# Layer norms by token halves in a five-layer transformer kernel

## The chip, the cores and the metric

The kernel runs on one core of one Trainium2 chip. The metric is the device time of one execution in microseconds (us), and the time given is the median of several executions.

TensorE (PE in the rows, its weight loads PEld) multiplies matrices, VectorE (DVE), ScalarE (ACT) and GpSimd (POOL) work on tiles, and SyncE (SP) issues transfers. Each works through its own list of instructions in order and waits at semaphores for the others.

## The reference

A first transformer block is followed by four more, all in float32 on 512 tokens of width 1024. What matters here is the frame of the four later layers:

```python
for i in range(4):
    h = x * (1 + scale[0]) + shift[0]
    y = mixer_i(h)                    # mLSTM, windowed attention, HGRN2, differential attention
    x = layer_norm(ALPHA * x + (1 + gate[0]) * y, ln_g[i, 0], ln_b[i, 0])
    h = x * (1 + scale[1]) + shift[1]
    y = (silu(h @ w_gate) * (h @ w_up)) @ w_down
    x = layer_norm(ALPHA * x + (1 + gate[1]) * y, ln_g[i, 1], ln_b[i, 1])

def layer_norm(x, g, b, eps=1e-5):    # over the 1024 channels of each token
    mu = x.mean(-1); var = square(x - mu).mean(-1)
    return (x - mu) * rsqrt(var + eps) * g + b
```

So there are eight layer norms: one after each output projection (the last step of `mixer_i`), one after each down projection. Each token is normed by itself, and each needs all 1024 channels of that token.

## The kernel before

**Layout.** Everything is kept transposed: 128 partitions hold channels, the free axis holds the 512 tokens. `x` has eight chunks `x[:, c, :]` of 128 channels (DT = 8). A result tile `m` of a projection is 128 output channels by 512 tokens in one of eight PSUM banks; tiles go round banks 0 to 3, and a tile may start when the one four before it has been evicted (`lin_free`).

**Products.** For float32 accuracy each operand is split in a high part of 32-bit matmul type and the rest. A chunk of a tile is three products, high by high, high by low, low by high (lines 756 to 758 in `slot_products`). A tile of the output projection has 8 chunks, so 24 products; one of the down projection has 22 chunks, so 66.

**Weights.** They come in slots of 8 chunks (512 KB): a DMA fills `raw`, ScalarE copies it to `w_hi` (L1440, `split`), GpSimd subtracts to get `w_lo` (L623, `low`). Each of the three has a ring of 4 slots (RING), and ScalarE may write a slot again when TensorE has used it (`slot_used`). An output or input tile has 1 slot, a down tile 3. ScalarE's list is written so that it splits 4 slots ahead (LEAD) of the tile in hand.

**Residual.** In `add_gated` VectorE adds each finished tile to `x` (L2062) and to a running sum over channels (L2066). ScalarE squares `x` (L1513), VectorE adds the squares (L2079), so that after the last tile little is left: add tile 7, square it, add the square.

**Layer norm.** `layer_norm` on TensorE sums over the partitions with a matrix of ones, one column per 128 tokens (L897, 8 float32 products, two records each). VectorE and ScalarE make mean, variance, root and inverse (L1988 to L1996, L1517), TensorE spreads the inverse and the mean times it over the partitions (L917, 8 products), VectorE multiplies (L1979) and subtracts (L1983) for each chunk of `x`. In between TensorE runs idle products (L903), which compute nothing. For each chunk ScalarE then writes `h_hi` (L1524) and `h_tmp` (L1526), and GpSimd `h_lo` (L661):

```python
act.wait_ge(sm.ln_y, (n["ln"] - 1) * DT + c + 1)
fn(h_hi[:, c, :], x[:, c, :], ACT.Identity, bias=..., scale=...).then_inc(sm.part_hi, 1)
fn(h_tmp[:, c, :], x[:, c, :], ACT.Identity, bias=..., scale=...).then_inc(sm.h_ready, 1)
```

**Early tiles.** The next projection does not wait for all of `h`. `early_tiles` runs the first three tiles (EARLY) together, chunk by chunk: six products with `h_hi[c]` (L854, L855), then three with `h_lo[c]` (L859). After its 16 writes ScalarE scales the residual in eight operations (L1530, `x_scaled`). Only behind these stand the next split of a slot (the one for tile 4) and, after an output projection, the table load and the first SiLU of the feed-forward part (L1800, in `ffn`). Tile 3 needs one slot more than the three early ones, and it is split right after the root.

The last norm of the program has no projection behind it: ScalarE writes `x` (L1537, `normed_output`), and each chunk is stored by a DMA of 256 KB.

**Third attention.** In the fourth layer `diff_attention` puts its scores in banks 1, 2 and 3 in turn, and the norm after it takes its sums in bank 0 (`NORM_SUMS[3]`).

Of the kernel before, what the change touches and what calls it, by code (L numbers as in the profile page):

```python
# [8 lines left out]
F32 = mybir.dt.float32  # L9
# [7 lines left out]
P = 128  # L17
S = 512
# [75 lines left out]
NORM_SUMS = {"first": 7, 0: 2, 3: 0}  # L94
# [69 lines left out]
PARTS_SPLIT = 3 * DT + FT  # L164

# [16 lines left out]
def lin_total(parts):  # L182

    return sum(len(IN_PROJ[p][0]) + len(IN_PROJ[p][1]) + 2 * DT + 2 * FT for p in parts)
# [34 lines left out]
def program(nc, xT, wstream, ada, cond, cols, kept, bigc, layerc, pos, yT, parts):  # L219
    slots_total = stream_length(parts)  # L220
    ctx = ExitStack()
    with ctx:
# [117 lines left out]
        def col(name, j=0, n=1):  # L340
# [37 lines left out]
                 "ln_var_done", "ln_root", "ln_inv", "ln_spread", "ln_times", "ln_y", "ln_x",  # L378
# [139 lines left out]
        LN_ORDER = [4, 0, 1, 2, 3, 5, 6, 7]  # L518
# [17 lines left out]
        def _(sp):  # L536
# [75 lines left out]
            for c in range(DT):  # L612
                if parts[-1] != "first":
                    sp.wait_ge(sm.ln_x, c + 1)
                sp.dma_start(yT[:, c, :], x[:, c, :]).then_inc(sm.stored, 16)
            sp.wait_ge(sm.stored, 16 * DT)
# [3 lines left out]
        def _(pool):  # L620
# [33 lines left out]
            def input_low(tile, scaled, chunks=range(DT)):  # L654

                for c in chunks:
                    n.add(part=1, h=1 if scaled else 0)
                    if scaled:
# [3 lines left out]
                                            ALU.subtract).then_inc(sm.part_lo, 1)  # L662

# [34 lines left out]
            for at, part in enumerate(parts):  # L698
# [6 lines left out]
                else:  # L705
# [10 lines left out]
                    else:  # L716
                        low_to(first_slot + LEAD)
                        input_low(lambda c: h_tmp[:, c, :], True)
# [19 lines left out]
                low_to(first_slot + inputs + DT + LEAD)  # L738
                input_low(lambda c: h_tmp[:, c, :], True)
# [6 lines left out]
        def _(pe):  # L746
# [124 lines left out]
            def residual_tiles(done, hi, lo, chunks, sums, parts_from=None):  # L871
# [3 lines left out]
                summed = 0  # L875
                for q in range(done, DT + 1):
# [7 lines left out]
                n.add(slot=(DT - done) * per, mt=DT - done)  # L884
# [9 lines left out]
            def token_sums(out, src):  # L894

                for t in range(TT):
                    op = mm(out[:, t:t + 1], src[:, t * P:(t + 1) * P], ones[:, 0:1], start=True, stop=True)  # L897
                return op
# [6 lines left out]
            def layer_norm(total, squares):  # L905

                pe.wait_ge(sm.lin_free, n["mt"] - 1)
                idle_products((n["mt"] - 2) % 4, 2)
                pe.wait_ge(sm.lin_free, n["mt"])
                token_sums(bank[6], total).then_inc(sm.ln_sum, 1)  # L910
                pe.wait_ge(sm.ln_moment, n["ln"])
                token_sums(bank[5], squares).then_inc(sm.ln_sum, 1)
                idle_products((n["mt"] - 1) % 4, 1)
                for at, src in enumerate((ln_rstd, ln_drop)):
                    pe.wait_ge(sm.ln_inv, 2 * n["ln"] - 1 + at)
                    for t in range(TT):
                        op = turn(bank[4 + 3 * at][:, t * P:(t + 1) * P], src[:, t:t + 1].to_broadcast([P, P]), ident)  # L917
                    op.then_inc(sm.ln_spread, 1)
                idle_products((n["mt"] - 1) % 4, 3)
# [142 lines left out]
            def diff_attention():  # L1062
                a, g, items = n["att"], n["att_g"], out_norms(3)
                for step in range(len(DF_UNITS) + 3):
                    if step < len(DF_UNITS):
                        hd, i = DF_UNITS[step]
                        w = (i + 1) * P
                        for c in range(2):
# [3 lines left out]
                            mm(bank[1 + (2 * step + c) % 3][:, 0:w], proj[:, hd, i * P:(i + 1) * P],  # L1072
# [297 lines left out]
            def ffn(sums):  # L1370
                early_tiles()
                linear(2 * FT - EARLY, h_hi, h_lo, [8])
                residual_tiles(0, hid_hi, hid_lo, [8, 8, 6], sums, parts_from=n["part"])
                n.add(part=FT)

            pe.wait_ge(sm.const_loaded, 48)
            for at, part in enumerate(parts):
# [8 lines left out]
                else:  # L1386
                    early_tiles()
                    if part == 0:
                        mlstm_gates()
                    linear(len(tiles) - EARLY, h_hi, h_lo, [8])  # L1390
# [24 lines left out]
                residual_tiles(EARLY, h_hi, h_lo, [8], sum_squares if part == "first" else pivot(sums_out[0]))  # L1415
                if part != "first":
# [1408 lines left out]
```

## Time and profile before

| | us |
|---|---|
| median of 3 runs | 3290.86 |
| lowest, highest | 3290.30, 3292.92 |
| profiled execution, its span | 3288.7 |
| TensorE busy in it | 3220.8 |
| VectorE, ScalarE, GpSimd busy | 1549.8, 1202.1, 1480.9 |

For the profiled execution the profile gives the span of the instructions, 3288.7 us, and no time of its own beside it. The span is 2.1 us under the median of the runs; what lies around the instructions is taken to be that.

Times in the rows below are microseconds from the start of the span, unless "mean ns" is said. In a timeline the first number is the start, the second the time from there to the end of the last instruction that the row joins (xN). A matmul's stated length is longer than its distance to the next, because matmuls overlap; the distance between starts is what it costs in a stream.

### The profile page before, as it was taken

Reading aid. Unit: us, or ns where it says so; the run is one execution under the profiler, and the core shown is the slowest. Engines: PE = TensorE matmul, PEld = TensorE weight load, DVE = VectorE, ACT = ScalarE, POOL = GpSimd, SP = SyncE. Lnnn points to the kernel's source line nnn. Section 1 sums busy time; section 2 is a strip of 40 time slices with the busy share of each in tenths; the row PEclk is TensorE's granted clock in tenths of the full one; section 3 lists DMA queues with packets and bytes.
Section 4 is the critical chain, followed back from the end, with each engine's and each line's share of the span. In section 5 each row is a group of like instructions: output and inputs, shape, how many; then the busy total and the mean of one; then the engine's idle time right before and its main releaser. Section 6 shows DMA issues by size and latency. Waiting matters only on the chain.

```text
span 3288.7 us, 42736 instructions
## 1 busy us (share of the span) xinstructions
PE 3220.8 (98%) x15181; PEld 2619.6 (80%) x15181; DVE 1549.8 (47%) x2615; ACT 1202.1 (37%) x1875; POOL 1480.9 (45%) x724
## 2 busy tenths in 40 slices
PE   8999999999999999999999999999999999999998
PEld 6876788888778888887888878877888877788886
DVE  2453355501145555467555224656556354752223
ACT  3455333222335332455432243125332243553322
POOL 3540554454235445524544454446444453154442
PEclk9999999999999999999999999999999999999999
DMA  4400155532224554211556333113555322032331
GB/s 161 122 26 1 65 204 191 202 106 93 68 65 160 193 202 145 84 59 63 180 191 208 105 96 96 39 33 103 204 191 188 103 90 77 5 99 96 96 103 64
DMA packets 103107, 376.12 MB, mean 114 GB/s; under 512 B 11456, under 2 KB 11584, under 8 KB 102848
## 3 DMA queue, kind: packets, MB, share of 16 engines
q1 hardware_dynamic: 102816, 373.86, 34.1%
q8 instruction: 81, 1.33, 0.2%
q0 software_dynamic: 160, 0.52, 0.1%
q14 instruction: 50, 0.41, 0.0%
HBM read 372.24 MB, written 2.10 MB: 114 GB/s over the span
## 4 chain that ended last, share of the span: by engine, by line
PE 52%; DVE 2%; ACT 1%; issue 1%; POOL 0%; DVEq 0%; ACTq 0%
PE bank L758 13%; PE bank L757 13%; PE bank L756 13%; PE bank L1362 2%; PE bank L859 1%; PE bank L854 1%; PE bank L855 1%; PE bank L808 1%; PE bank L809 1%; PE bank L810 1%; PE bank L1072 1%; PE bank L1328 1%; PE bank L1089 0%; PE bank L974 0%; PE bank L1258 0%
## 5 line engine op out<-in xcount | busy, mean ns | idle before, releaser
L623 POOL TENSOR_TENSOR w_lo<-raw,w_hi 128x1024 fp32r<-128x1024 f32 x501 | 1227.3, 2455 | 1368.2 <-ACT w_hi L1440 1368.0
L1440 ACT ACTIVATE w_hi<-raw 128x1024 fp32r<-128x1024 f32 x501 | 526.8, 1057 | 1183.2 <-PE bank L758 1022.4
L756 PE MATMUL bank<-h_hi,w_hi 128*128 128x512 f32 x2280 | 889.3, 390 | 0.0
L758 PE MATMUL bank<-h_hi,w_lo 128*128 128x512 f32 x2280 | 887.1, 389 | 0.0
L757 PE MATMUL bank<-h_lo,w_hi 128*128 128x512 f32 x2280 | 887.0, 389 | 0.0
L756 PEld LDWEIGHTS bank<-h_hi,w_hi 128*128 128x128 f32 x2280 | 427.9, 188 | 90.6 <-issue 2.0
L757 PEld LDWEIGHTS bank<-h_lo,w_hi 128*128 128x128 f32 x2280 | 427.9, 188 | 89.7 <-issue 1.0
L758 PEld LDWEIGHTS bank<-h_hi,w_lo 128*128 128x128 f32 x2280 | 427.9, 188 | 89.2
L2608 DVE CUSTOM_DVE_ANT_0 ada_raw<-ada_raw,cond_row 128x1024 f32<-128x1024 f32 x192 | 304.2, 1587 | 280.5 <-DMA ada_raw<-ada 270.6
L756 PE MATMUL bank<-hid_hi,w_hi 128*128 128x512 f32 x880 | 344.0, 391 | 0.0
L758 PE MATMUL bank<-hid_hi,w_lo 128*128 128x512 f32 x880 | 342.4, 389 | 0.0
L757 PE MATMUL bank<-hid_lo,w_hi 128*128 128x512 f32 x880 | 342.4, 389 | 0.0
L2624 DVE TENSOR_TENSOR hid_lo<-layer_const,hid_hi 128x512 f32 (+1 forms) x110 | 228.0, 2073 | 108.5 <-ACT hid_hi L1805 108.5
L661 POOL TENSOR_TENSOR h_lo<-proj,h_hi 128x512 fp32r<-128x512 f32 x40 | 55.7, 1407 | 308.5 <-ACT h_hi L1472 308.5
L757 PEld LDWEIGHTS bank<-hid_lo,w_hi 128*128 128x128 f32 x880 | 165.2, 188 | 35.3 <-issue 1.0
L756 PEld LDWEIGHTS bank<-hid_hi,w_hi 128*128 128x128 f32 x880 | 165.2, 188 | 35.1 <-issue 1.0
L758 PEld LDWEIGHTS bank<-hid_hi,w_lo 128*128 128x128 f32 x880 | 165.2, 188 | 34.3
L1800 ACT ACTIVATE layer_const<-bank 128x512 f32<-128x512 f32 x110 | 65.7, 597 | 321.1 <-PE bank L758 317.0
L2062 DVE SCALAR_TENSOR_TENSOR x<-bank,mod,x 128x512 f32<-128x512 f32 x64 | 48.0, 750 | 264.4 <-PE bank L758 255.7
L2621 DVE TENSOR_TENSOR layer_const<-bank,layer_const 128x512 f32<-128x512 f32 x110 | 75.9, 690 | 201.0 <-PE bank L758 163.4
L854 PE MATMUL bank<-h_hi,w_hi 128*128 128x512 f32 x336 | 135.5, 403 | 1.3 <-ACT h_hi L1472 1.0
L855 PE MATMUL bank<-h_hi,w_lo 128*128 128x512 f32 x336 | 131.9, 393 | 0.0
(411 smaller groups left out, 4016.5 us busy)
## 6 DMA issues: line engine op xcount, KB each, us to landing
raw<-weights SPq DMA_DIRECT2D x501, 512.0 KB, 3.5
ada_raw<-ada SPq DMA_DIRECT2D x192, 512.0 KB, 4.3
layer_const<-layer_const SPq DMA_DIRECT2D x5, 512.0 KB, 3.6
x<-x_t SPq DMA_DIRECT2D x1, 2048.0 KB, 7.5
cond_row<-cond SPq DMA_DIRECT2D x4, 512.0 KB, 4.2
y_t<-x SPq DMA_DIRECT2D x8, 256.0 KB, 2.0
tables<-big_const SPq DMA_DIRECT2D x1, 768.0 KB, 5.9
cols<-columns SPq DMA_DIRECT2D x1, 569.5 KB, 8.4
```

The source lines that it names most:

```text
L623: nc.gpsimd.tensor_tensor(w_lo[k % RING][:, :, :], raw[k % RING][:, :, :], w_hi[k % RING][:, :, :].bitcast(F32), ALU.subtract).then_inc(sm ...
L756: mm(out, w_hi[r][:, at, :], hi, start=first and at == 0, stop=False)
L757: mm(out, w_hi[r][:, at, :], lo, start=False, stop=False)
L758: op = mm(out, w_lo[r][:, at, :], hi, start=False, stop=last and at == len(pairs) - 1)
L854: mm(out, w_hi[r][:, c, :], h_hi[:, c, :], start=c == 0, stop=False)
L855: mm(out, w_lo[r][:, c, :], h_hi[:, c, :], start=False, stop=False)
L1362: op = mm(bank[3 + m % 3][:, j * P:(j + 1) * P], kk[:, j * P:(j + 1) * P], qq[:, j * P:(j + 1) * P], start=True, stop=True)
L1440: fn(w_hi[t % RING][:, :, :], raw[t % RING][:, :, :], ACT.Copy).then_inc(sm.hi_done, 1)
L1800: fn(sil[q % 2], bank[(mt + 2 * q) % 4][:, :], ACT.Silu).then_inc(sm.sil_done, 1)
L2608: v.tensor_tensor_reduce(w, w, cond_row[:, :], 1.0, 0.0, ALU.mult, ALU.add, ada_part[:, kc:kc + 1]).then_inc(sm.ada_used, 1)
L2621: v.tensor_tensor(sil[q % 2], bank[(mt + 2 * q + 1) % 4][:, :], sil[q % 2], ALU.mult).then_inc(sm.lin_free, 2)
L2624: v.tensor_tensor(hid_lo[:, q + 4 * i, :], sil[q % 2], hid_hi[:, q + 4 * i, :].bitcast(F32), ALU.subtract).then_inc(sm.part_lo, 1)
```

## The change

1. Tokens are cut into two halves of 256. The last tile (7) of an output or down projection is computed as two half tiles, first all chunks for tokens 0 to 255, then all chunks for tokens 256 to 511 (`half_tile`), in two banks.
2. The norm of half 0 stands inside the second half tile on TensorE: after chunk 3, 7 and 8 (output) or 6, 12 and 13 (down) come the sums and the two spreads. The idle products go, but for the last norm of the program.
3. The three early tiles are run by halves (`early_halves`): eight chunks for half 0, then eight for half 1. For chunks 0 to 2 of half 0 only two tiles are run, the third tile catches up after chunk 2. After chunk 3 of half 0 TensorE makes the sums of half 1, after chunk 5 its spreads.
4. ScalarE, VectorE and GpSimd do the norm by halves: 32 writes of `h` with 256 columns in place of 16 with 512, 32 of VectorE's operations in place of 16, 16 of GpSimd's in place of 8. Each has a fixed order in which both halves' steps, and the splits of slots, are mixed.
5. The residual is scaled as before, 8 times 512 columns, after all 32 writes.
6. The output is stored in 16 DMAs of 128 KB in place of 8 of 256 KB.
7. Since each norm's last tile now takes two banks, the count of tiles shifts; in the fourth layer the scores go to banks 0, 1 and 3 and the sums to bank 2.

The core of the diff (waits and signals of other functions left out):

```diff
-NORM_SUMS = {"first": 7, 0: 2, 3: 0}
+NORM_SUMS = {"first": 7, 0: 2, 3: 2}
+TAIL = {"out": (7,), "down": (7,)}
...
+            def half_tile(k, mt, hi, lo, chunks, half, after=lambda: None):
+                cols = half_cols(half)
+                out = bank[mt % 4][:, cols]
...
+                    for at in range(m):
+                        mm(out, w_hi[r][:, at, :], hi[:, c, cols], start=c == 0, stop=False)
+                        mm(out, w_hi[r][:, at, :], lo[:, c, cols], start=False, stop=False)
+                        op = mm(out, w_lo[r][:, at, :], hi[:, c, cols], start=False, stop=c == last)
+                        if half == 1 and at == m - 1:
+                            op.then_inc(sm.slot_used, 1)
...
+                        at = (6, 12, 13) if per > 1 else (3, 7, 8)
+                        if passed == at[0]:
+                            half_sums(0, tail, *norm)
+                        elif passed in at[1:]:
+                            half_spread(0, at.index(passed) - 1)
...
+            def early_halves(tail, total, squares):
...
+                        if half == 0 and c == LN_CHUNK - 1:
+                            for before in range(LN_CHUNK):
+                                high(0, before, EARLY - 1)
+                                low(0, before, EARLY - 1)
+                        if half == 0 and c == 3:
+                            half_sums(1, tail, total, squares)
+                        if half == 0 and c == 5:
+                            for at in range(2):
+                                half_spread(1, at)
...
+            def normed_low(first):                      # GpSimd
+                low_to(first + 2)
+                half_low(0)
+                low_to(first + 3)
+                for c in range(1, DT):
+                    half_low(c)
+                low_to(first + LEAD)
+                for c in range(DT):
+                    later_low(c)
...
+                for _ in tail:                          # ScalarE, end of layer_norm
+                    square()
+                root(0)
+                split_ahead(1)
+                apply(0, 0)
+                if slots > 1:
+                    split_ahead(1)
+                apply(0, 1)
+                square()
+                for c in (2, 3):
+                    apply(0, c)
+                root(1)
+                for c in range(4, DT):
+                    apply(0, c)
+                if slots > 1:
+                    split_ahead(1)
+                for c in range(DT):
+                    apply(1, c)
...
+                second_half(7)                          # VectorE, end of add_gated
+                for c in (3, 4):
+                    apply(0, c)
+                moments(1)
+                apply(0, 5)
+                inverses(1)
+                apply(0, 6)
+                apply(0, 7)
+                for c in range(DT):
+                    apply(1, c)
...
-                            mm(bank[1 + (2 * step + c) % 3][:, 0:w], proj[:, hd, i * P:(i + 1) * P],
+                            mm(bank[(0, 1, 3)[(2 * step + c) % 3]][:, 0:w], proj[:, hd, i * P:(i + 1) * P],
```

**ScalarE at the first output projection's norm.** Before: `bank<-x` are the squares, `ln_small` the root, `w_hi` a split, `h_hi` and `h_tmp` the writes of `h`, in brackets the semaphores waited for.

```order
L1440 ACTIVATE w_hi_59<-raw_55 128x1024 [waits slot_used,raw_loaded1]
L1513 ACTIVATE bank<-x 128x512 [waits ln_added,ln_residual] x2
L1517 ACTIVATE ln_small<-ln_small,kept 128x4 [waits ln_var_done]
L1440 ACTIVATE w_hi_60<-raw_56 128x1024 [waits slot_used,raw_loaded2]
L1524 ACTIVATE h_hi<-x,ln_cols 128x512 [waits ln_y]
```

The same place after the change, from the root of half 0 to that of half 1 (`sq_88` is the square of the last tile's second half):

```order
L1695 ACTIVATE ln_small<-ln_small,kept 128x2 [waits ln_var_done]
L1613 ACTIVATE w_hi_60<-raw_56 128x1024 [waits slot_used,raw_loaded2]
L1731 ACTIVATE h_hi<-x,ln_cols 128x256 [waits ln_y]
L1733 ACTIVATE h_tmp<-x,ln_cols 128x256
L1731 ACTIVATE h_hi<-x,ln_cols 128x256 [waits ln_y]
L1733 ACTIVATE h_tmp<-x,ln_cols 128x256
L1688 ACTIVATE sq_88<-x 128x256 [waits ln_residual]
L1731 ACTIVATE h_hi<-x,ln_cols 128x256 [waits ln_y]
L1733 ACTIVATE h_tmp<-x,ln_cols 128x256
L1731 ACTIVATE h_hi<-x,ln_cols 128x256 [waits ln_y]
L1733 ACTIVATE h_tmp<-x,ln_cols 128x256
L1695 ACTIVATE ln_small<-ln_small,kept 128x2 [waits ln_var_done]
```

A second root now stands between the fourth and the fifth pair of writes, and the 24 other writes stand behind it.

**GpSimd at the same norm.** Before, the slots 0, 1 and 2 of the early tiles and slot 3 are all made low before the first `h_lo`:

```order
L623 TENSOR_TENSOR w_lo_62<-raw_54,w_hi_58 128x1024 [waits hi_done]
L622 REGISTER_ALU
L623 TENSOR_TENSOR w_lo_63<-raw_55,w_hi_59 128x1024 [waits hi_done]
L622 REGISTER_ALU
L623 TENSOR_TENSOR w_lo_64<-raw_56,w_hi_60 128x1024 [waits hi_done]
L199 REGISTER_ALU
L199 COMPARE_AND_BRANCH
L661 TENSOR_TENSOR h_lo<-h_tmp,h_hi 128x512 [waits part_hi,h_ready] x8
```

After (here `w_lo_65` and `w_lo_62` are the slots of the first two early tiles, `w_lo_63` that of the third, `w_lo_64` that of tile 3):

```order
L654 TENSOR_TENSOR w_lo_65<-raw_57,w_hi_61 128x1024 [waits hi_done]
L654 TENSOR_TENSOR w_lo_62<-raw_54,w_hi_58 128x1024 [waits hi_done]
L701 TENSOR_TENSOR h_lo<-h_tmp,h_hi 128x256 [waits half_hi,half_tmp]
L654 TENSOR_TENSOR w_lo_63<-raw_55,w_hi_59 128x1024 [waits hi_done]
L701 TENSOR_TENSOR h_lo<-h_tmp,h_hi 128x256 [waits half_hi,half_tmp] x7
L654 TENSOR_TENSOR w_lo_64<-raw_56,w_hi_60 128x1024 [waits hi_done]
L710 TENSOR_TENSOR h_lo<-h_tmp,h_hi 128x256 [waits part_hi,h_ready] x8
```

The low part of the third early tile's slot has moved behind the first half chunk, that of tile 3's slot behind the eighth.

## Rows read from the trace of the kernel before

**Rows 1.** The page: engines over the whole span; shares of the chain.

```profile
PE 3220.8 (98%) x15181; PEld 2619.6 (80%) x15181; DVE 1549.8 (47%) x2615; ACT 1202.1 (37%) x1875; POOL 1480.9 (45%) x724
PE 52%; DVE 2%; ACT 1%; issue 1%; POOL 0%; DVEq 0%; ACTq 0%
```

**Rows 2.** Windows, the seven norms with a projection behind: length, then engines, clock.

```profile
995.02:1003.66 8.64, 8.31 (x37) 5.81 (x36) 5.73 (x13) 3.28 (x6) 2.36 (x1) 0.80 0.39 137
...
1550.47:1558.03 7.56, 7.18 (x38) 4.54 (x36) 5.17 (x12) 2.71 (x5) 2.32 (x1) 1.00 0.40 156
...
sum 55.84, PE 53.59 PEld 35.32 DVE 37.57 ACT 20.39 POOL 16.34; mean PE 7.66 PEld 5.05 DVE 5.37 ACT 2.91 POOL 2.33
```

**Rows 3.** Timeline of TensorE, second layer's output norm.

```profile
1550.24 0.39 PE L758 MATMUL bank<-h_hi,w_lo 128*128 128x512 f32 x1
...
1552.14 1.95 PE L897 MATMUL bank<-kept,sums_out 128*128 128x1 f32 x16 [0.21 <-DVE sums_out L2066]
...
1558.03 0.50 PE L854 MATMUL bank<-h_hi,w_hi 128*128 128x512 f32 x1
```

**Rows 4.** Timeline of VectorE, same norm: a square added, a subtraction.

```profile
1548.74 0.69 DVE L2079 TENSOR_TENSOR sums_out<-sums_out,bank 128x512 f32<-128x512 f32 x1
...
1550.67 0.75 DVE L2062 SCALAR_TENSOR_TENSOR x<-bank,mod,x 128x512 f32<-128x512 f32 x1 [1.24 <-PE bank L758]
```

**Rows 5.** Timeline of ScalarE, same norm, from the first write of h.

```profile
1557.16 0.81 ACT L1524 ACTIVATE h_hi<-x,ln_cols 128x512 fp32r<-128x512 f32 x1 [1.52 <-DVE x L1983]
...
1568.48 5.75 ACT L1530 ACTIVATE x<-x,ln_cols 128x512 f32<-128x512 f32 x8
1574.24 1.28 ACT L1800 ACT_TABLE_LOAD   x1
1575.54 0.60 ACT L1800 ACTIVATE layer_const<-bank 128x512 f32<-128x512 f32 x1
1576.03 2.00 ACT L1440 ACTIVATE w_hi<-raw 128x1024 fp32r<-128x1024 f32 x2
```

**Rows 6.** Timeline of GpSimd, same norm.

```profile
1558.76 12.83 POOL L661 TENSOR_TENSOR h_lo<-h_tmp,h_hi 128x512 fp32r<-128x512 f32 x8 [0.68 <-ACT h_tmp L1526]
1577.16 7.58 POOL L623 TENSOR_TENSOR w_lo<-raw,w_hi 128x1024 fp32r<-128x1024 f32 x3 [5.57 <-ACT w_hi L1440]
```

**Rows 7.** Window of the same norm's three early tiles.

```profile
1558.03:1575.20 17.17, 16.75 (x73) 13.54 (x73) 12.20 (x17) 17.15 (x24) 12.20 (x9) 1.00 0.18 62
```

**Rows 8.** Groups by form over the span: busy, mean ns of one | idle before.

```profile
L1615 ACT ACTIVATE df_p<-df_p,small 128x512 f32<-128x512 f32 x16 | 11.3, 711 | 0.0
L1615 ACT ACTIVATE df_p<-df_p,small 128x256 f32<-128x256 f32 x16 | 7.9, 496 | 0.0
L2342 DVE TENSOR_TENSOR st_e<-st_z,bank 128x256 f32<-128x256 f32 x4 | 1.7, 414 | 0.0
L649 POOL TENSOR_TENSOR hg_k<-hg_k,hg_pow 128x128 f32<-128x128 f32 x8 | 3.4, 427 | 3.0 <-PE bank L1356 3.0
```

**Rows 9.** TensorE: products of 256 columns, of 128 columns, and the page's weight load.

```profile
131.20 0.28 PE L1153 MATMUL bank<-w_hi,blk_parts 128*64 128x256 f32 x1
131.32 0.28 PE L1153 MATMUL bank<-w_lo,blk_parts 128*64 128x256 f32 x1
...
1432.27 0.27 PE L826 MATMUL bank<-w_lo,h_hi 128*128 128x128 f32 x1
1432.38 0.28 PE L827 MATMUL bank<-w_hi,h_lo 128*128 128x128 f32 x1
...
L756 PEld LDWEIGHTS bank<-h_hi,w_hi 128*128 128x128 f32 x2280 | 427.9, 188 | 90.6 <-issue 2.0
```

**Rows 10.** Timeline of ScalarE, second layer's down norm, after its writes.

```profile
1936.83 5.74 ACT L1530 ACTIVATE x<-x,ln_cols 128x512 f32<-128x512 f32 x8
1943.31 2.96 ACT L1440 ACTIVATE w_hi<-raw 128x1024 fp32r<-128x1024 f32 x3 [0.74 <-PE bank L859]
```

**Rows 11.** Timeline of ScalarE, last norm: the last write before its store.

```profile
3285.48 0.81 ACT L1537 ACTIVATE x<-x,cols 128x512 f32<-128x512 f32 x1 [0.51 <-DVE x L1983]
```

More of the change, by code:

```diff
@@ L182, in lin_total @@
 def lin_total(parts):
-    return sum(len(IN_PROJ[p][0]) + len(IN_PROJ[p][1]) + 2 * DT + 2 * FT for p in parts)
+    return sum(len(IN_PROJ[p][0]) + len(IN_PROJ[p][1]) + 2 * DT + 2 * FT +
+               (0 if p == "first" else len(TAIL["out"]) + len(TAIL["down"])) for p in parts)
 class Counts(dict):
@@ L869, in early_tiles, with residual_tiles @@
                 early_done()
-            def residual_tiles(done, hi, lo, chunks, sums, parts_from=None):
+            def half_tile(k, mt, hi, lo, chunks, half, after=lambda: None):
+                cols = half_cols(half)
+                out = bank[mt % 4][:, cols]
+                pe.wait_ge(sm.lin_free, mt - 3)
+                c, last = 0, sum(chunks) - 1
+                for s, m in enumerate(chunks):
+                    if half == 0:
+                        pe.wait_ge(sm.lo_done, k + s + 1)
+                    r = (k + s) % RING
+                    for at in range(m):
[4 more added lines that the diff above has]
+                            op.then_inc(sm.slot_used, 1)
+                        if half == 0 and c == last:
+                            op.then_inc(sm.half_tile, 1)
+                        c += 1
+                        after()
+            def residual_tiles(done, hi, lo, chunks, sums, parts_from=None, tail=(), norm=None):
                 k, mt, per = n["slot"], n["mt"], len(chunks)
-                summed = 0
-                for q in range(done, DT + 1):
+                summed, whole = 0, DT - len(tail)
+                for q in range(done, whole if tail else DT + 1):
                     if q < DT:
@@ L892, in pivot, with token_sums @@
                 return add
-            def token_sums(out, src):
-                for t in range(TT):
-                    op = mm(out[:, t:t + 1], src[:, t * P:(t + 1) * P], ones[:, 0:1], start=True, stop=True)
+            def token_sums(out, sources, half):
+                for t in range(2):
+                    for at, src in enumerate(sources):
+                        op = mm(out[:, 2 * half + t:2 * half + t + 1], src[:, t * P:(t + 1) * P], ones[:, 0:1],
+                                start=at == 0, stop=at == len(sources) - 1)
                 return op
```

372 lines of the change are left out of this document (250 added, 122 removed).

## The prediction

> **What bounds the kernel now.** I read the page first. TensorE is busy for 98% of the span and the chain that ended last is mostly its own [rows 1], so the end moves only where TensorE computes nothing of use, or gets to compute less. Idle products count as busy, so that share hides the norms. The windows between the last product of a last tile and the first early product show them: seven, 55.84 us together, 7.56 each with the clock granted in full and about 8.6 in the three in which 0.80 was granted [rows 2]. The early tiles behind a norm take 17.17 us [rows 7], where 72 products at a distance of 0.227 (24 of them fill the 5.46 us of a tile) make 16.4. An eighth norm ends the program. So some 60 us are there to be had. What could take their place is read from ScalarE: in the early tiles it was busy for 17.15 of 17.17 us [rows 7]. It has no room there, and what it does next, scaling the residual, ends with the table load at the very moment when it is wanted [rows 5].
>
> **Prices.** A norm is followed in us from Ta, the start of the last tile: 1545.01 in the second layer's output projection, which is the last product's start plus 0.23 less 5.46 [rows 3]. Half products: the trace has 256 columns at a distance of 0.12 and, with weights of 128 columns, 128 columns at 0.11 [rows 9]; I take 0.114, so that two halves cost no more than a whole. ScalarE: the eight operations of 5.75 us start 0.707 apart and last 0.80 [rows 5]; its form of 256 columns is 0.215 shorter than that of 512 [rows 8], so a half write is 0.59 long and 0.49 apart. That puts 32 of them at 15.8 us, against 16 × 0.707 = 11.3. Bounds: 0.35 if all of the cost went with the columns, 0.55 if a third of the saving were missing; I take 0.49, since the measured pair of forms has just this step. VectorE: 256 columns 0.41 [rows 8], a pair of multiply and subtract about 0.79; 16 pairs 12.6 us, in the shadow of ScalarE. GpSimd: 128 columns 0.43 [rows 8], 512 unhindered 1.30 (8 of them span 12.83 us, ScalarE's pace in between [rows 6]), so 0.74 for 256; bounds 0.65, half of 1.30, and 0.90. A slot's low part 2.4 (three in 7.58 us [rows 6]). Float32 sums: 16 records in 1.95 us [rows 3], 0.112 each; a half's 6 products have 12, so 1.3 us, and both spreads of a half 0.44. TensorE thus does 2 × (1.3 + 0.44) = 3.5 us of norm work that it cannot overlap with products; this takes the place of the idle ones and of waiting.
>
> ScalarE's price is also one that the Trainium skill states: "ScalarE: Activation LUTs", section What ACT_TABLE_LOAD costs, has an operation with pointers for bias and scale at 372 ns plus 0.833 ns a column, less 93 ns when back to back. By it a half write is 0.585 long and 0.492 apart; the trace has 0.80 for 512 columns, where the rule gives 0.799. It speaks against halving: each cut in two buys 0.28 us of fixed cost again.
>
> **An output norm.** 2.74: half tile 0 is done. VectorE is not there yet: it adds tile 6's square until 1549.43, or 4.4 [rows 4]. Two half additions (0.48 long, 0.40 apart) end at 5.2; TensorE, which stands before the sums with three chunks of half 1 made, has waited 1.5 for them. Sums to 6.6, 15 products and the spreads to 8.8. ScalarE's next split waits for the tile's slot, free only at the end of half 1: 8.7 to 9.7. Then it starts to write `h`: 9.7 against 12.15 before [rows 5]. That is all that is won, 2.4 us.
> ScalarE reaches the second root at 13.9 (four pairs, one square). That root waits for the sums of half 1, which TensorE makes behind chunk 3. Chunk 1 needs its `h_lo`, and on GpSimd the third early tile's slot stands ahead of it: chunk 0's `h_lo` ends at 11.6, the slot at 14.0, chunk 1 at 14.7. TensorE has waited 2.5. Then chunks 1 to 3 and the third tile's nine products run to 17.9, the sums to 19.2, the variance to 19.5: ScalarE has stood for 5.6. TensorE waits 1.25 until chunk 4 comes, 0.6 for its `h_lo`, and again 1.6 at the start of half 1, where GpSimd has tile 3's slot (24.6 to 27.0) ahead of the `h_lo`. The early tiles end at 35.5, against 30.2 before.
> ScalarE, in order: 9.7 + 15.8 of writes + 0.5 square and root + 5.6 + 0.7 (its wait for the spreads) = 32.3. Then eight residuals 5.66, to 38.0; the table load 1.28, to 39.3, no longer hidden; SiLU 0.49; the split for tile 4, 1.05, to 40.8; its low part 2.4, to 43.3. TensorE ended tile 3 at 35.5 + 5.46 = 41.0 and waits 2.3. Before, tile 4 began at 1580.64, or 35.6. So 7.7 us slower; in the two output norms with the clock at 0.80, where it began about 0.6 later, 7.1. Behind it nothing gives it back: the feed-forward part is TensorE's at 5.46 a tile. Four such norms: 2 × 7.7 + 2 × 7.1 = 29.6.
>
> **A down norm.** Its tile has 66 products, 15.0 us, and VectorE is free. Half 0 ends at 7.5; its sums, wanted 2.05 later, are ready for, and its norm hides behind half 1, which ends at 16.8 with 1.8 of sums and spreads in it. ScalarE writes the first half chunk at 14.4, before the tile is done. Three splits now lie between its steps, each behind a slot that half 1 has to free. GpSimd's low part of the third slot (16.5 to 18.9) again holds up chunk 1, by 1.75, ScalarE stands for 4.6 at the second root, and TensorE waits 1.25 for chunk 4, 0.6, and 1.8 at half 1's first `h_lo`. The early tiles end at 40.6 (39.7 before). ScalarE: 14.4 + 15.8 + 0.5 + two splits 1.9 + 4.6 + 0.2 = 37.5; residuals to 43.2, split to 44.2, low part to 46.7. Before, ScalarE's residuals were over 0.74 us ahead of need [rows 10], and tile 4 began at 45.2. So 1.5 slower, 1.0 in the norm with the lower clock: 2 × 1.5 + 1.0 = 4.0.
>
> **The last norm.** Before, the last write starts 16.6 us after the last tile's last product and 3.3 before the end [rows 11]. Now half 1 ends 1.8 later, VectorE does two left pairs (1.6), moments and three pairs more before half 1's eight (6.3); the last write ends at Ta + 29.7, in place of Ta + 32.4. The stores are half as large but twice as many; the last alone counts, and I price it as before (bounds: 1 us less, half the transfer; 1 us more, queued behind others). So 2.7 gained.
>
> **Banks of the third attention**, the shifted tile banks, the waits added before the residuals (on ScalarE's own signals): nothing, since the same number of banks turn in the same order. If a bank were shared with a running tile, one eviction, 0.7 us, would come in.
>
> Sum: 29.6 + 4.0 − 2.7 = 30.9 us on the span of 3288.7; with the 2.1 us between span and median, 3290.9 + 31 = 3322 us.
>
> **Rivals.**
> A, faster. The waits of ScalarE at the second root do not come, because the sums of half 1 are there when it is. Then the output norm's tile 4 begins at 43.3 − 6.3 = 37.0, 1.4 slower or 0.8; a down norm is bound by TensorE, 16.8 + 16.4 + 1.8 + 5.46 = 40.5, rounded up by one wait of 0.5 to 41.0, so 4.2 faster; with the last norm 4.4 − 13.1 − 2.7, or about −11: 3280. For it: VectorE and ScalarE do start earlier. Against it: the order on GpSimd, written into its list.
> B, slower by less. The early tiles end late as worked out, but residuals, SiLU and the split find room: only 2 × 5.3 + 2 × 4.7 + 2.2 (down) − 2.7 = 19.5 remain: 3310. Against it stands that ScalarE was without slack before.
> C, slower by more. The clock falls to 1.2 GHz in these scattered waits, as in the three norms at 0.80, or VectorE's work slows GpSimd's half chunks to 0.90. A stretch at 0.80 was 1.0 us longer [rows 2]; twice in seven norms 14: 3336.
> D. A weight load is not hidden behind a half product. Then half products pass 0.188 apart [rows 9] in place of 0.114: 192 of them in an output norm, 14 us, 276 in a down norm, 20, and 132 at the end, 10; together 126, of which some 20 fill waits. That gives 3322 + 105 = 3427. This is what the Trainium skill would have, "TensorE: Matmul & The Clock Gate", section The mechanism: loads overlap running products only when they are in other row groups. The trace speaks against it: full loads with 128 columns pass 0.11 apart.
>
> **How the numbers follow.** Forecast 0.56, with its own range 3312 to 3332: the bounds of a half write move an output norm by −2 and +1 and a down norm by −2 and +1.5, those of GpSimd by up to 1. A 0.12, B 0.14, C 0.16, D 0.02. The range that should hold the time 8 times in 10 reaches over most of B and C: 3302 to 3341. What this kernel's measurement can tell from no change is about 0.2%, or 6.6 us: faster by more, 0.10 (most of A); within it, 0.05 (A's rest and a bit of B); slower, 0.85.
>
> **What would show it.** ScalarE's half writes about 0.49 apart; its second root behind 4 to 6 us of idle; GpSimd's low part of the third slot between the first and the second half chunk, and TensorE idle for 2 us before the second `h_lo`; residual operations that end after the early tiles; a wait of TensorE for `w_lo` before tile 4 in each feed-forward part. I am wrong if tile 4 starts within 1 us of the end of tile 3, or if the early tiles behind an output norm end less than 31 us after Ta.

## The result, and the profile after

The changed kernel takes 3351.7 us (median of 4 runs, 3347.9 to 3353.1), the kernel before 3290.6 in the same session: a ratio of 1.0186, 95% interval 1.0171 to 1.0200, +61 us. I had forecast 3322, +31, with a range up to 3341. The sign and the place were right, the size was half.

The page of the profiled execution (span 3346.1), the lines that answer to [rows 1]:

```profile
PE 3234.1 (97%) x16021; PEld 2677.5 (80%) x16021; DVE 1563.5 (47%) x2791; ACT 1241.9 (37%) x2011; POOL 1487.1 (44%) x780
...
PE 48%; DVE 3%; ACT 2%; issue 2%; POOL 1%; DVEq 0%; POOLq 0%; ACTq 0%
```

TensorE is busy for 13 us more and the span is 57 us longer; so it waits, and part of its work is slower. The next windows go from Ta, the start of the last tile, to the start of tile 4. Columns: length, busy time of PE, PEld, DVE, ACT, POOL, granted clock, DMA share, GB/s; `...` stands where rows are left out. First the second layer's output norm and down norm, the sum of all seven, then a stretch inside the output norm.

```profile
1558.76:1606.64 47.88, 39.11 (x249) 36.36 (x247) 24.22 (x59) 31.88 (x56) 22.65 (x21) 0.85 0.16 56
1931.38:1979.91 48.53, 44.58 (x334) 42.57 (x332) 20.74 (x55) 31.15 (x53) 23.65 (x22) 0.96 0.18 55
...
sum 336.73, PE 288.50 PEld 270.98 DVE 163.47 ACT 221.03 POOL 160.19; mean PE 41.21 PEld 38.71 DVE 23.35 ACT 31.58 POOL 22.88
...
1565.52:1582.00 16.48, 12.47 (x68) 11.64 (x68) 6.02 (x19) 5.91 (x13) 5.12 (x5) 0.70 0.19 65
```

Before, this output norm took 35.6 and the down norm 45.2. The stretch at 0.70 is new: in the kernel before the clock was granted in full there [rows 2, 7].

TensorE in that output norm (last half product before the sums, the sums, half 1 behind them, the first early product, its waits for chunk 1's `h_lo` and for chunk 4, then the end of tile 3 and tile 4):

```profile
1562.60 0.28 PE L946 MATMUL bank<-h_hi,w_lo 128*128 128x256 f32 x1
1564.01 0.83 PE L998 MATMUL bank<-kept,sums_out 128*128 128x1 f32 x6 [1.14 <-DVE sums_out L2279]
...
1565.88 0.41 PE L945 MATMUL bank<-h_lo,w_hi 128*128 128x256 f32 x1
1566.09 0.41 PE L946 MATMUL bank<-h_hi,w_lo 128*128 128x256 f32 x1
...
1570.86 0.38 PE L1046 MATMUL bank<-h_hi,w_hi 128*128 128x256 f32 x1 [1.48 <-ACT h_hi L1731]
...
1575.18 0.80 PE L1051 MATMUL bank<-h_lo,w_hi 128*128 128x256 f32 x2 [1.37 <-POOL h_lo L701]
...
1582.55 0.58 PE L1046 MATMUL bank<-h_hi,w_hi 128*128 128x256 f32 x1 [1.15 <-ACT h_hi L1731]
...
1603.66 0.39 PE L820 MATMUL bank<-h_hi,w_lo 128*128 128x512 f32 x1
1606.64 0.79 PE L818 MATMUL bank<-h_hi,w_hi 128*128 128x512 f32 x1 [2.59 <-POOL w_lo L654]
1607.23 0.63 PE L819 MATMUL bank<-h_lo,w_hi 128*128 128x512 f32 x1
```

Up to 1562.60 half products pass 0.12 apart. Then TensorE stands for 1.14, makes sums of one column, and the next half products pass 0.21 apart (1565.88 to 1566.09): that is the level of 1.2 GHz. The same happens behind the 2.59 us before tile 4, whose first products are 0.4 to 0.6 apart instead of 0.227.

ScalarE, from the first write of `h`; the row at 1587.60 is the first write of half 1, the last row is the second root of the second layer's down norm:

```profile
1570.22 0.59 ACT L1731 ACTIVATE h_hi<-x,ln_cols 128x256 fp32r<-128x256 f32 x1
1570.71 0.59 ACT L1733 ACTIVATE h_tmp<-x,ln_cols 128x256 f32<-128x256 f32 x1
...
1581.71 0.30 ACT L1695 ACTIVATE ln_small<-ln_small,kept 128x2 f32<-128x2 f32 x1 [7.13 <-DVE ln_small L2207]
...
1587.60 0.60 ACT L1731 ACTIVATE h_hi<-x,ln_cols 128x256 fp32r<-128x256 f32 x1 [1.64 <-DVE x L2197]
...
1595.54 5.76 ACT L1741 ACTIVATE x<-x,ln_cols 128x512 f32<-128x512 f32 x8
1601.32 1.28 ACT L2011 ACT_TABLE_LOAD   x1
1602.61 0.60 ACT L2011 ACTIVATE layer_const<-bank 128x512 f32<-128x512 f32 x1
1603.11 2.00 ACT L1613 ACTIVATE w_hi<-raw 128x1024 fp32r<-128x1024 f32 x2
...
1956.58 0.30 ACT L1695 ACTIVATE ln_small<-ln_small,kept 128x2 f32<-128x2 f32 x1 [4.50 <-DVE ln_small L2207]
```

This is the chain of the forecast: half writes 0.59 long and 0.49 apart, a root that waits, residuals behind the writes, then table load, SiLU and the split for tile 4, none of them hidden any longer [rows 5].

GpSimd in the output norm: chunk 0's low part, the slot's, chunks 1 to 3; and the last three of half 1.

```profile
1571.38 0.73 POOL L701 TENSOR_TENSOR h_lo<-h_tmp,h_hi 128x256 fp32r<-128x256 f32 x1 [9.74 <-ACT h_tmp L1733]
1572.07 2.38 POOL L654 TENSOR_TENSOR w_lo<-raw,w_hi 128x1024 fp32r<-128x1024 f32 x1
1574.40 2.10 POOL L701 TENSOR_TENSOR h_lo<-h_tmp,h_hi 128x256 fp32r<-128x256 f32 x3
...
1593.73 3.79 POOL L710 TENSOR_TENSOR h_lo<-h_tmp,h_hi 128x256 fp32r<-128x256 f32 x3 [0.26 <-ACT h_tmp L1733]
```

The last write of the program, against [rows 11], 2.7 us before the end of the span and 29.85 after its Ta of 3313.53:

```profile
3343.38 0.60 ACT L1748 ACTIVATE x<-x,cols 128x256 f32<-128x256 f32 x1 [0.19 <-DVE x L2197]
```

**Where the 57.4 us between the two spans lie.** From Ta to tile 4: output norms +10.2, +12.2, +12.7, +12.2, together 47.3; down norms +2.9 to +3.5, together 9.8. The feed-forward parts behind tile 4 took 324.7 to 324.9 us instead of 323.2: 6.5, the slow first products of tile 4. Last norm −2.2. All other stretches −4.0: −2.7 before the first of these norms, +1.8 and −3.3 in the attention and HGRN2 layers, where single stretches at the lower clock come and go from one execution to the next. The fourth layer's stage with the swapped banks took 233.4 against 233.2.

### The profile page after: what moved, and what is told of

Same layout as the page of the kernel before. It is cut to its first block, busy times and chain, and to the rows that moved or that the text cites. A ratio compares the mean times of both kernels' runs of the same rounds, so it can differ in the third digit from the quotient of the medians.

```text
span 3346.1 us, 44788 instructions
## 1 busy us (share of the span) xinstructions
PE 3234.1 (97%) x16021; PEld 2677.5 (80%) x16021; DVE 1563.5 (47%) x2791; ACT 1241.9 (37%) x2011; POOL 1487.1 (44%) x780
## 4 chain that ended last, share of the span: by engine, by line
PE 48%; DVE 3%; ACT 2%; issue 2%; POOL 1%; DVEq 0%; POOLq 0%; ACTq 0%
PE bank L818 11%; PE bank L820 11%; PE bank L819 11%; PE bank L1524 2%; PE bank L870 1%; PE bank L872 1%; PE bank L1234 1%; PE bank L871 1%; ACT h_hi L1731 1%; ACT h_tmp L1733 1%; PE bank L944 1%; PE bank L946 1%; PE bank L945 1%; PE bank L921 1%; PE bank L916 1%
## 5 line engine op out<-in xcount | busy, mean ns | idle before, releaser
L818 PE MATMUL bank<-h_hi,w_hi 128*128 128x512 f32 x2248 | 880.6, 392 | 15.1 <-POOL w_lo L654 15.1
L820 PE MATMUL bank<-h_hi,w_lo 128*128 128x512 f32 x2248 | 876.6, 390 | 0.0
L818 PE MATMUL bank<-hid_hi,w_hi 128*128 128x512 f32 x792 | 309.7, 391 | 0.0
L820 PE MATMUL bank<-hid_hi,w_lo 128*128 128x512 f32 x792 | 308.2, 389 | 0.0
L819 PE MATMUL bank<-hid_lo,w_hi 128*128 128x512 f32 x792 | 308.2, 389 | 0.0
L819 PEld LDWEIGHTS bank<-hid_lo,w_hi 128*128 128x128 f32 x792 | 148.7, 188 | 31.9 <-issue 1.0
L820 PEld LDWEIGHTS bank<-hid_hi,w_lo 128*128 128x128 f32 x792 | 148.6, 188 | 30.9
L2276 DVE SCALAR_TENSOR_TENSOR x<-bank,mod,x 128x512 f32<-128x512 f32 (+1 forms) x72 | 49.7, 690 | 235.0 <-PE bank L820 199.1
L1046 PE MATMUL bank<-h_hi,w_hi 128*128 128x256 f32 x336 | 97.9, 313 | 13.6 <-ACT h_hi L1731 13.6
L2016 ACT ACTIVATE hid_hi<-layer_const 128x512 f32 (+1 forms) x110 | 68.3, 621 | 94.9 <-DVE layer_const L2869 94.9
```

Of the source, the lines that this page charges most:

```text
L818: mm(out, w_hi[r][:, at, :], hi, start=first and at == 0, stop=False)
L819: mm(out, w_hi[r][:, at, :], lo, start=False, stop=False)
L820: op = mm(out, w_lo[r][:, at, :], hi, start=False, stop=last and at == len(pairs) - 1)
L1046: mm(out, w_hi[r][:, c, :], h_hi[:, c, cols], start=c == 0, stop=False)
L2016: fn(hid_hi[:, q + 4 * i, :], sil[q % 2], ACT.Copy).then_inc(sm.part_hi, 1)
```

## The experiments

Twelve kernels, each timed beside the kernel before. Differences to the changed kernel are taken across sessions; the median of the kernel before was 3289.8 to 3290.6 in all of them. The columns out and down are the time from Ta to tile 4 in the second layer's output and down norm. The edits are shown abridged.

| kernel | out | down | median, us | ratio to before (95%) |
|---|---|---|---|---|
| before | 35.6 | 45.2 | 3290 | |
| changed | 47.9 | 48.5 | 3351.7 | 1.0186 (1.0171 to 1.0200) |
| idle | 59.5 | 54.8 | 3412.5 | 1.0377 (1.0362 to 1.0391) |
| resid | 45.4 | 47.2 | 3328.5 | 1.0115 (1.0100 to 1.0131) |
| root | 45.8 | 44.5 | 3327.2 | 1.0116 (1.0101 to 1.0132) |
| all3 | 58.2 | 54.7 | 3404.9 | 1.0350 (1.0335 to 1.0364) |
| fill | 43.8 | 47.9 | 3326.5 | 1.0113 (1.0097 to 1.0128) |
| rr | 43.2 | 45.1 | 3316.0 | 1.0086 (1.0072 to 1.0099) |
| rrgf | 38.8 | 44.2 | 3295.4 | 1.0014 (1.0005 to 1.0023) |
| noidle | 36.9 | 47.7 | 3300.4 | 1.0033 (1.0021 to 1.0046) |
| down0 | 36.4 | 48.2 | 3298.0 | 1.0025 (1.0016 to 1.0035) |
| down1 | 35.9 | 44.2 | 3287.4 | 0.9990 (0.9981 to 0.9999) |
| pool | 47.5 | 52.2 | 3358.3 | 1.0210 (1.0197 to 1.0224) |
| all4 | 38.0 | 44.4 | 3293.7 | 1.0012 (1.0003 to 1.0021) |

My theory after the result: the chain was as forecast, and what I had not priced is the clock, which the removed idle products had kept. The rivals: the halves cost more everywhere, or one of the waits in the chain is much worse than worked out.

**idle.**

```diff
+    idle_products(bank that is free, FILL[...])   # 384 columns, ahead of five waits of a norm
```

> The changed kernel with idle products (384 columns, nothing computed) in the waits that its trace shows: in an output norm 6 before the sums of half 0, 8 before the first early product, 7 before chunk 1's low part, 6 before chunk 4, 14 before tile 4; in a down norm 7, 6 and 7 at the last three. Theory 1, the fallen clock costs the part I had not priced: granted clock stays at 1.00 in the output norms, ScalarE's wait at the second root falls from 7.1 to about 4, half products pass 0.12 apart everywhere, tile 4 starts 3.4 earlier and itself runs 1.7 faster: about 3330. Rival, the half products and waits at ScalarE's pace lower the clock whatever stands between them, or the pace of ScalarE alone counts: 3346 to 3355.

Measured 3412.5, 61 us slower. I had mis-sized the filler. The window of the second output norm:

```profile
1578.22:1637.68 59.46, 59.06 (x332) 46.54 (x330) 25.92 (x60) 33.09 (x57) 29.09 (x23) 1.00 0.22 75
```

The clock is 1.00 as expected, but TensorE is busy for all 59 us: each product stands as two records 0.32 apart, 0.645 us, and 41 of them are 26 us in place of the five waits' 7.7 us in this norm (1.14, 1.48, 1.37, 1.15 and 2.59). So the clock can be held; of the time this kernel says nothing. The same holds for all3.

**resid.**

```diff
 with up to q = 3 of the first round of SiLUs unrolled:
     up(q, 0)
+    scaled_residual((2 * q, 2 * q + 1))
 next layer: for c in range(DT):
     split_ahead(1)
+    scaled_residual((c,))
```

> The changed kernel with the eight scalings of the residual spread behind the next splits, two by two behind SiLUs in the feed-forward part, one behind each split of the next layer's input projection, so that SiLU and split for tile 4 follow the last half write directly. Theory 1: the wait before tile 4 (2.6 in an output norm, 3.4 in the last, 1.3 in a down norm) goes, and with it the dip of the clock at its end (1.7 in an output norm): 3351.7 - 10.4 - 3.9 - 6.8, about 3331. Rival, the split waits for the slot that the early tiles free, and its low part behind it is late all the same: over 3345.

Measured 3328.5, −23. TensorE at the start of tile 4 (1602.16) no longer waits:

```profile
1601.93 0.39 PE L820 MATMUL bank<-h_hi,w_lo 128*128 128x512 f32 x1
1602.16 0.41 PE L818 MATMUL bank<-h_hi,w_hi 128*128 128x512 f32 x1
```

So the wait before tile 4 is ScalarE's residual standing ahead of the split, as predicted. In the traces tile 4 comes 8.5 us earlier over the four output norms and 4.4 over the three down norms, and itself takes 5.5 instead of 7.0 behind an output norm. The clock in the output norms stayed low (0.85 in three, 0.78 in the fourth), so apart from tile 4's own 1.5 us this gain is the chain's, not the clock's.

**root.**

```diff
-    if half == 0 and c == 3:     # sums of half 1
+    if half == 0 and c == 1:
-    if half == 0 and c == 5:     # its spreads
+    if half == 0 and c == 4:
```

> The changed kernel with TensorE's sums of half 1 behind chunk 1 of half 0 in place of chunk 3, its spreads behind chunk 4 in place of 5. Theory 1, ScalarE stands at the second root only because the sums are so far back in TensorE's list: that wait falls from 7.1 to about 2.5 and everything ScalarE does later, tile 4 too, comes 4 earlier in output norms and 1 earlier in down norms: about 3332. Rival, chunk 1 is held up by GpSimd, and TensorE's own products and waits set the end of the early tiles: gain under 5, so over 3346.

Measured 3327.2, −24.5. The second root of the same output norm:

```profile
1570.65 0.30 ACT L1695 ACTIVATE ln_small<-ln_small,kept 128x2 f32<-128x2 f32 x1 [4.08 <-DVE ln_small L2207]
```

7.13 has become 4.08 (I expected 2.5), and tile 4 comes 2.1 earlier there and 4.0 in the down norm, where I expected 1. So at least 3 of the 7.1 us were the place of the sums in TensorE's list. Here too the output norm's clock stayed at 0.85.

**all3.**

```diff
+ the edits of idle, resid and root
```

> The three edits together (idle products, residual spread, sums of half 1 earlier). Theory 1, each removes its own wait and TensorE's own work is what is left: tile 4 at about 37 after the start of the last tile in output norms (48 now, 35.6 before the change) and 44 in down norms (48.6 now, 45.2 before): about 3292, equal to the kernel before. Rival, the waits replace one another, so that the gains don't add: 3310 to 3325.

Measured 3404.9: idle's excess again, 7.7 us better than idle. It tells nothing of the sum of the three.

**fill.**

```diff
 against the kernel idle:
-FILL = {"out": (6, 8, 7, 6, 14), "down": (0, 0, 7, 6, 7)}, 384 columns
+FILL = {"out": (3, 4, 4, 3, 7), "down": (0, 0, 4, 3, 3)}, 192 columns
```

> The changed kernel with idle products again, now sized by what the kernel idle's trace shows (0.645 us for one of 384 columns, so 41 of them were 26 us per output norm against 8.4 us of waits): 192 columns, 0.32 each; 3, 4, 4, 3 and 7 in an output norm, 0, 0, 4, 3 and 3 in a down norm, so never longer than the wait that they stand in. Theory 1, the clock stays in full in the waits and costs nothing: tile 4 starts near 44.5 in output norms (47.9 in the changed kernel) and runs at the full clock: about 3332. Rival, ScalarE's pace alone sets tile 4: 3346 or more.

Measured 3326.5, −25.2, with nothing but idle products added to the changed kernel. The second output norm's window, then ScalarE's first write there, its second root, and the first write of half 1:

```profile
1556.49:1600.33 43.84, 40.81 (x291) 37.69 (x289) 23.78 (x59) 31.75 (x56) 22.59 (x21) 1.00 0.19 61
```

```profile
1566.40 0.58 ACT L1749 ACTIVATE h_hi<-x,ln_cols 128x256 fp32r<-128x256 f32 x1
...
1576.27 0.30 ACT L1713 ACTIVATE ln_small<-ln_small,kept 128x2 f32<-128x2 f32 x1 [5.54 <-DVE ln_small L2225]
...
1581.34 0.60 ACT L1749 ACTIVATE h_hi<-x,ln_cols 128x256 fp32r<-128x256 f32 x1 [0.83 <-DVE x L2215]
```

The clock is 1.00 in all four output norms, each takes 43.8 to 43.9, and ScalarE waits for 5.54: the forecast had 43.3 and 5.6. This is the experiment that settles the size.

**rr.**

```diff
+ the edits of resid and root
```

> The changed kernel with the two edits that gained apart: residual spread, and the sums of half 1 behind chunk 1. Theory 1, the two waits are separate ones in the same chain of ScalarE and what is left before tile 4 in the kernel root (2.44 in an output norm, 0.3 in a down norm, and the clock behind it) goes: 3327.2 - 9.8 - 1 - 6.8, about 3310. Rival, the earlier sums have already made that room: 3322 to 3328.

Measured 3316.0, −35.7 against the changed kernel, where the two apart give −47.7. In the output norm they add (47.9 to 45.4 and 45.8 apart, 43.2 together); but either one already lets tile 4 behind an output norm run in 5.5 or 5.6 instead of 7.0, and the three down norms gain 10.3 together, where the two apart give 4.4 and 10.7: in root two of them had the clock at 1.00 (44.5), here all three have 0.96 (45.1).

**rrgf.**

```diff
 GpSimd:   half_low(0), half_low(1), half_low(2)
+          low_to(first + 3)                       # was behind half_low(0)
 TensorE:  LN_CHUNK = 4; sums of half 1 behind chunk 0, spreads behind chunk 3
+          idle products of 192 columns: out (3, 4, 4), down (3)
```

> The kernel rr and three edits more: sums of half 1 behind chunk 0 and its spreads behind chunk 3; on GpSimd the low part of the third early slot behind chunk 2's half instead of chunk 0's, the third tile catching up behind chunk 3; idle products of 192 columns, 3 and 4 and 4 in an output norm, 3 in a down norm. Theory 1, ScalarE's second root then waits for nothing and its writes alone set the end of the early tiles: tile 4 at 39 to 40 in output norms, 43 in down norms, 3290 to 3297. Rival, VectorE or GpSimd is the next to be late in each norm: over 3303.

Measured 3295.4, within theory 1's range. The output norms take 37.8, 38.8, 38.8 and 37.8 (the clock at 1.00 in the first and last, at 0.96 in the other two), less than the 39 to 40 expected; the down norms take 44.2, not 43. ScalarE in the second output norm, second root and first write of half 1:

```profile
1562.67 0.30 ACT L1713 ACTIVATE ln_small<-ln_small,kept 128x2 f32<-128x2 f32 x1
...
1569.75 0.60 ACT L1749 ACTIVATE h_hi<-x,ln_cols 128x256 fp32r<-128x256 f32 x1 [2.05 <-DVE x L2220]
```

The root waits for nothing worth a mark; a wait of 2.05 has come up at the first write of half 1, whose spreads TensorE makes behind chunk 3.

**noidle.** The kernel before, with less.

```diff
-                idle_products((n["mt"] - 2) % 4, 2)
-                idle_products((n["mt"] - 1) % 4, 1)
-                idle_products((n["mt"] - 1) % 4, 3)
```

> The kernel before without the six idle products of each layer norm (they compute nothing). Theory 1, they keep the clock: each of seven norms then shows a half-clock stretch of some 3.4 us in its early tiles, 1.5 each: about 3300. Rival, the clock does not hang on them (or ScalarE's pace hides it): 3288 to 3292.

Measured 3300.4, +10.0. The gap and the early tiles of the second output norm, against 7.56 at 1.00 [rows 2] and 17.17 at 1.00 [rows 7]:

```profile
1552.30:1560.43 8.13, 4.04 (x25) 3.43 (x25) 5.16 (x12) 2.71 (x5) 2.35 (x1) 0.77 0.38 144
1560.43:1578.34 17.91, 17.91 (x72) 14.69 (x73) 12.21 (x17) 17.73 (x25) 12.15 (x8) 0.91 0.18 59
```

Products that compute nothing were worth 10 us over eight norms. Over the seven norms the early tiles take 129.3 against 118.9.

**down0.** One part of the change alone.

```diff
-TAIL = {"out": (7,), "down": (7,)}
+TAIL = {"out": (), "down": (7,)}     # output norms and their early tiles by whole tiles, as before
```

> One part alone: the three down norms and the last one by halves as in the changed kernel, the four output norms by whole tiles as in the kernel before (banks of the third attention shifted to fit). Theory 1, the loss sits in the output norms as the start of tile 4 says (47.3 us of it there, 9.8 in the down norms, -2.2 at the end): 3290.3 + 9.8 - 2.2, about 3298. Rival, the loss belongs to the halves in general (TensorE's pitch, the shared clock): over 3310.

Measured 3298.0, +8 over before where the trace gave 7.6. So 54 of the 61 us come with the output norms.

**pool.**

```diff
 GpSimd:   half_low(0), half_low(1), half_low(2)
+          low_to(first + 3)                       # was behind half_low(0)
 TensorE:  LN_CHUNK = 4
```

> The changed kernel with GpSimd's order alone changed: the low part of the third early slot behind chunk 2's half (before: behind chunk 0's), the third tile catching up behind chunk 3. Theory 1, the wait of 1.4 before chunk 1 only moves to chunk 3, the sums of half 1 stand behind that chunk still, and ScalarE's second root waits about as long: 3345 to 3353. Rival, as I had predicted it, GpSimd's 2.4 us in front of chunk 1 hold up everything behind it: some 2 us in each of seven norms, 3337.

Measured 3358.3, 6.5 slower than the changed kernel: both theories failed. The second root of the second down norm:

```profile
1967.84 0.29 ACT L1695 ACTIVATE ln_small<-ln_small,kept 128x2 f32<-128x2 f32 x1 [7.87 <-DVE ln_small L2207]
```

It waited for 4.50 in the changed kernel. The sums of half 1 still stand behind chunk 3. In this down norm TensorE's wait of 1.34 before chunk 1's `h_lo` has moved to chunk 3 and become 2.02, and the 12 products of the third tile between it and the sums pass 0.21 apart, at the level of 1.2 GHz. From Ta to tile 4 the four output norms change by +1.0, −0.4, −2.3 and 0, the three down norms by +3.3 to +3.7. Whether GpSimd's order helps where the sums don't stand behind it was tried only together with other edits, in rrgf.

**all4.**

```diff
-    if half == 0 and c == 3:     # rrgf: spreads of half 1
+    if half == 0 and c == 2:
     idle products: out (3, 4, 2) instead of (3, 4, 4), down (2) instead of (3)
```

> The kernel rrgf with the spreads of half 1 behind chunk 2 in place of chunk 3 and two idle products fewer. In rrgf's trace ScalarE stands for 2.05 us at the first write of half 1, since VectorE waits for these spreads. Theory 1, that wait goes and tile 4 of an output norm starts near 37: 3289. Rival, GpSimd's low part of the fourth slot, just ahead of half 1's first, or TensorE is the bound now: 3294 to 3296.

Measured 3293.7. The second output norm went from 38.8 to 38.0, not to 37; over all four it is 0.9 less, since the first and the last went up from 37.8 to 38.2, and a down norm takes 0.2 more: nearer to the rival. 1.8 us under rrgf is at the limit of what these runs can tell.

**down1.** The version that the experiments point to: halves where they pay, whole tiles where they don't.

```diff
 down0, and the edits of rrgf (residual, sums, GpSimd's order, three idle products in a down norm)
```

> As down0, with what helped in rrgf: residual spread behind the splits (in both kinds of norm), sums of half 1 behind chunk 0 and spreads behind chunk 3, GpSimd's slot behind chunk 2's half, three idle products of 192 columns. By rrgf's trace tile 4 starts 44.2 after the start of the last tile in a down norm (45.2 to 45.7 in the kernel before), the last norm is 2.2 shorter: 3290.3 - 3.5 - 2.2, about 3284.5, and faster than both kernels. Rival, the output norms lose by the residual spread what the down norms win: 3290 or more.

Measured 3287.4 over 11 runs (3280.0 to 3290.9), ratio 0.9990, interval 0.9981 to 0.9999: faster than the changed kernel by 64 us, than the kernel before by a bare 2.4, where I expected 5.8; the interval all but touches 1. Its three down norms:

```profile
1350.36:1394.61 44.25, 43.58 (x339) 42.12 (x338) 24.04 (x59) 27.11 (x47) 25.32 (x22) 1.00 0.21 65
...
sum 132.72, PE 130.71 PEld 126.34 DVE 68.55 ACT 81.34 POOL 75.95; mean PE 43.57 PEld 42.11 DVE 22.85 ACT 27.11 POOL 25.32
```

132.7 for three, against 136.0 before, with the clock at 1.00: that gain came. In the trace the four output norms take 1.5 more than before, with the clock at 0.95 in three of them instead of two; whether the missing 3.4 us went there, the spread between executions (11 us in down1, 9 in before) hides.

## Why the prediction was wrong in size

**The step that failed** is in the part on prices: "TensorE thus does 2 × (1.3 + 0.44) = 3.5 us of norm work that it cannot overlap with products; this takes the place of the idle ones and of waiting." I counted the idle products as time given back, and the sum, 29.6 + 4.0 − 2.7, puts the clock that they kept at nothing. It measured 25 us: put back where the new waits are, idle products of 192 columns bring the clock in the output norms (0.85 to 0.88 in the changed kernel) back to 1.00 and the time from 3351.7 to 3326.5 (fill). In the kernel before, taking them out costs 10 us (noidle). Rival C named the mechanism, but its price came from the wrong rows: 1.0 us for a gap at 0.80 [rows 2], twice in seven norms, 14 us. In that gap little is computed. Here the low clock falls on half products that ScalarE is waiting for, and on the first products of tile 4. Of the 4.0 us by which fill's second output norm is shorter, 1.6 come at ScalarE's first write (9.9 after Ta instead of 11.5), 1.6 at its second root (5.54 instead of 7.13) and 0.8 at the first write of half 1 (0.83 instead of 1.64). In the two traces an output norm is 2.5 to 4.6 us shorter to tile 4 with fill, and the feed-forward part behind it 1.4.

The Trainium skill, "TensorE: Matmul & The Clock Gate", section HAM oscillation — how this bites in real kernels, prices a throttled stretch at half its length. Products agree nearly (0.213 against 0.120 apart); but the wait of ScalarE behind them carries it on into the chain, and tile 4 moves by it.

**What held, with the clock in full (fill).** First write 9.9 after Ta (9.7 forecast), second root's wait 5.5 (5.6), early tiles' end 35.9 (35.5), residuals from 32.75 (32.3), tile 4 at 43.85 (43.3). Half writes 0.49 apart. In a down norm root wait 4.5 (4.6), early end 41.6 (40.6), tile 4 at 47.9 (46.7). The banks cost 0.2 us at most. Fill is +36 us over before, the forecast was +31: the output norms take 31.8 more (29.6 forecast), the down norms 7.7 (4.0), the last norm 2.2 less (2.7). So the second term that was too small is the down norm, 2.6 each instead of 1.5 (1.0 in one).

**Smaller terms.**
- TensorE's idle before the second `h_lo` was 1.37 in the changed kernel's second output norm, 2.03 in the fourth, where I had 2.5; in fill that `h_lo` was taken up 14.9 after Ta, against 14.7.
- Half products pass 0.120 apart, not 0.114; 256 columns stood at 0.12 in [rows 9], and I leaned to a value that made two halves equal a whole. With 276 of them up to the end of the early tiles this is up to 1.7 us in a down norm, and there the half tile did end late: 17.5 instead of 16.8, and the early tiles 1.0 late.
- GpSimd's halves of half 0 take 0.73 as forecast; those of half 1 a mean of 0.83, up to 1.7 beside VectorE's first two operations for the next layer's modulation (3.79 us for three, above); that these are the cause was not tried. My 0.74 was right, but a straight line between the rows used, 0.43 and 1.30, gives 0.72, and a third of the saving missing gives 0.56 for a half write, not 0.55; neither slip moves the forecast.
- Last norm −2.2 instead of −2.7: the last write ended at Ta + 30.45 instead of 29.7, and the end followed it 2.1 later, 0.3 sooner than before, within the bounds given for the store.
- The half writes cost what was worked out, so halving bought little: the output norm's first write comes 2.2 earlier, and 32 writes take 4.5 longer than 16.

**The rivals.** A fell: the waits at the second root came. Its condition can be made, though: in rrgf the root doesn't wait, and then an output norm takes 37.8 to 38.8, not the 37.0 that A had, and a down norm 44.2, not 41.0. B fell: the residual found no room (resid gains 23). D fell: half products pass 0.120 apart, not 0.188. The rule of the Trainium skill that loads overlap only products in other row groups ("TensorE: Matmul & The Clock Gate", section The mechanism) is not what this trace shows; the same section also lets a load into a background weight buffer go ahead of running products, and 0.120 does not contradict that. C was right as to the cause and too small by nearly half (14 us, where fill shows 25).

## What to carry to other kernels

Before you count filler work as waste, ask what it keeps: waits of 0.6 to 1.5 us on TensorE, with one-column sums between them, went with 0.70 of its clock over 16 us, and idle products in these waits brought back 1.00. The products behind such waits run slower, and whoever waits for those products pays too. When work is cut finer to start earlier, follow the engine that issues it in order, since a fixed price per operation and one item placed ahead of the next need can eat the head start. Halving paid, by 3.3 us over three norms and barely in the whole, where a tile has 66 products to hide a norm behind (down1), and not where it has 24 (rrgf, +9.5 over four).

## What the runs showed of the hardware

- Float32 products of 384 columns are two records of 0.32 us each, so one costs 0.645 (kernel idle): filler has to be sized by its own rows (idle against fill, 86 us).
- With 32-bit matmul types, 512 columns pass 0.227 apart and 256 pass 0.120; 0.0133 a product does not scale with columns.
- A tiny VectorE operation of two columns, 0.16 us otherwise, took 1.2 to 1.3 in all seven norms of rrgf, where GpSimd was in a slot's low part (1562.39 to 1564.78), and likewise in the seven of all4 and the three down norms of down1; each time it ended within 0.03 us of GpSimd's operation; the inverse just before it, beside the same low part, took 0.16. In the changed kernel, where the two don't meet, it never took longer. Why was not tried.

```profile
1562.39 2.39 POOL L655 TENSOR_TENSOR w_lo<-raw,w_hi 128x1024 fp32r<-128x1024 f32 x1
...
1563.34 0.16 DVE L2237 RECIPROCAL ln_small<-ln_small 128x2 f32<-128x2 f32 x1
1563.53 1.27 DVE L2239 SCALAR_TENSOR_TENSOR ln_small<-ln_small 128x2 f32<-128x2 f32 x1
```
